# Value panels of attention and memory: two k-tiles of 512 channels in each, four panels adding up in two banks

## The reference, cut to what matters

```python
h = rms_norm(x, norm_w[layer])
proj = jnp.einsum('bsd,de->bse', h, w_in[layer])
(gq, gk, gv, glr, hq, hf, hi, xq, gate) = jnp.split(proj, split_idx, axis=-1)
...
gla_o = chunked_gated_linear_attention(..., split_heads(gv, GLA_HEADS), ...)
hgrn_o = chunked_gated_linear_attention(..., split_heads(hi, HGRN_HEADS), ...)
m = rms_norm(mem, mem_norm_w[layer])
mkv = jnp.einsum('bmd,de->bme', m, w_mem_kv[layer])
mk, mv = jnp.split(mkv, 2, axis=-1)
...
mixed = jnp.concatenate([gla_o, hgrn_o, xo], axis=-1) * jax.nn.silu(gate)
x = x + jnp.einsum('bse,ed->bsd', mixed, w_out[layer])
```

## Time and profile before

| | |
|---|---|
| median of 3 runs | 996.04 us (995.47 to 996.21) |
| profiled execution, its own time | 996.28 us |
| its span | 994.5 us |
| PE busy | 978.4 us (98%), 8087 matmul records |
| PEld busy | 962.3 us (97%) |
| DVE, ACT, POOL busy | 546.6, 492.0, 749.5 us |
| granted PE clock | full (2.4 GHz) in all but the last slice |
| chain that ended last | PE 87%, DVE 6%, ACT 3%, POOL 2% |

### The profile page before, as it was taken

How to read it: one execution, slowest core, us unless ns; L and a number is a source line. 1 busy time by engine, 2 the same in 40 slices (tenths; PEclk the granted TensorE clock), 3 DMA queues, 4 the chain that set the end, 5 groups by cost and what they waited for, 6 DMA issues and landing times.

```text
span 994.5 us, 21475 instructions
## 1 busy us (share of the span) xinstructions
PE 978.4 (98%) x8087; PEld 962.3 (97%) x8087; DVE 546.6 (55%) x976; ACT 492.0 (49%) x767; POOL 749.5 (75%) x586
## 2 busy tenths in 40 slices
PE   9999999999999999999999999999999999999996
PEld 7999999999999999999899899999999999999996
DVE  4945994457644444701783885456647564445113
ACT  6634335456554444544566754532264665454441
POOL 2896757656999888999289855666549549999993
PEclk9999999999999999999999999999999999999998
DMA  9563334343565555566365243443226736666561
GB/s 317 177 195 131 122 126 148 128 128 106 178 194 185 173 169 169 165 180 182 113 187 154 81 128 108 128 128 123 90 86 191 233 108 197 201 191 178 179 182 53
DMA packets 48346, 154.50 MB, mean 155 GB/s; under 512 B 6060, under 2 KB 11188, under 8 KB 48280
## 3 DMA queue, kind: packets, MB, share of 16 engines
q1 hardware_dynamic: 46128, 151.20, 48.9%
q10 hardware_dynamic: 2152, 2.38, 0.7%
HBM read 151.46 MB, written 2.10 MB: 154 GB/s over the span
## 4 chain that ended last, share of the span: by engine, by line
PE 87%; DVE 6%; ACT 3%; POOL 2%; DMA 1%; issue 1%; SPq 0%; DVEq 0%; ACTq 0%; POOLq 0%
PE panel L1846 70%; PE panel L1912 3%; POOL wlo L662 1%; DMA memk<-in_mem_panels 1%; PE aux L2013 1%; PE panel L1883 1%; PE aux L2291 1%; PE aux L2280 1%; PE panel L1948 1%; PE aux L2253 1%; PE aux L2321 1%; PE aux L2330 1%; DVE tmp L1248 1%; PE aux L1920 1%; PE aux L2019 1%
## 5 line engine op out<-in xcount | busy, mean ns | idle before, releaser
L662 POOL TENSOR_TENSOR wlo<-raw,whi 128x512 fp32r<-128x512 f32 x546 | 724.7, 1356 | 222.8 <-ACT whi L759 194.5
L1846 PE MATMUL panel<-xh,whi 128*128 128x256 f32 (+2 forms) x1392 | 400.4, 288 | 1.0 <-POOL wlo L662 0.7
L1846 PE MATMUL panel<-xh,wlo 128*128 128x256 f32 (+2 forms) x1392 | 394.9, 284 | 0.0
L1846 PE MATMUL panel<-xl,whi 128*128 128x256 f32 (+2 forms) x1392 | 394.6, 283 | 0.0
L759 ACT ACTIVATE whi<-raw 128x1024 fp32r<-128x1024 f32 x280 | 293.9, 1054 | 192.4 <-PE panel L1846 155.5
L1846 PEld LDWEIGHTS panel<-xh,whi 128*128 128x128 f32 x1392 | 262.7, 189 | 2.2 <-POOL wlo L662 1.2
L1846 PEld LDWEIGHTS panel<-xh,wlo 128*128 128x128 f32 x1392 | 262.8, 189 | 0.0
L1846 PEld LDWEIGHTS panel<-xl,whi 128*128 128x128 f32 x1392 | 262.0, 188 | 0.2
L1846 PE MATMUL panel<-hh,wlo 128*128 128x272 f32 (+1 forms) x352 | 100.5, 286 | 0.0
L1846 PE MATMUL panel<-hh,whi 128*128 128x272 f32 (+1 forms) x352 | 100.2, 285 | 0.0
L1846 PE MATMUL panel<-hl,whi 128*128 128x272 f32 (+1 forms) x352 | 99.9, 284 | 0.0
(11 more groups left out here) (363 smaller groups left out, 1619.2 us busy)
## 6 DMA issues: line engine op xcount, KB each, us to landing
raw<-in_panels SPq DMA_DIRECT2D x232, 512.0 KB, 3.5
raw<-in_down SPq DMA_DIRECT2D x32, 448.0 KB, 3.3
raw<-in_down SPq DMA_DIRECT2D x16, 512.0 KB, 3.6
memk<-in_mem_panels SPq DMA_DIRECT2D x4, 512.0 KB, 7.7
memx<-in_mem SPq DMA_DIRECT2D x4, 256.0 KB, 5.6
h<-in_x SPq DMA_DIRECT2D x1, 1024.0 KB, 8.6
spill<-h ACTq DMA_DIRECT2D x1, 1024.0 KB, 5.1
h<-spill ACTq DMA_DIRECT2D x1, 1024.0 KB, 6.5
```

What stands on the lines that cost most here:

```text
L662: ins = nc.gpsimd.tensor_tensor(wlo[:, slot, half], raw[:, slot, half], whi[:, slot, half].bitcast(f32), ALU.subtract)
L1846: ins = M(bank[:, 0:w], wt[:, slot, P * t:P * t + P], x[:, kk, c0:c0 + w], start=first and m == 0 and n == 0, stop=last and m == len(pairs ...
```

## The change

A value panel now holds two k-tiles of 512 channels. Four such panels make a group: `part` 0 to 3 brings k-tiles 2·part and 2·part+1, and the group's 512 channels add up in two banks, one for each `rt`, over the whole width of a bank. There are three groups of attention's values and one of the memory's. Each panel has 12 matmuls with 512 moving columns and counts as a pass of its own. The banks are emptied by two 512-column instructions behind the fourth panel. The list `FIRST` is the same. `value_banks` gives the group's banks (0 and 1, then 2 and 3, then 0 and 1), `frees` and the increments of 2 keep the counts of the banks that are skipped, and `mk`'s tiles are drained in the order 2, 3, 0, 1. Steps ("o", i) wait for `value_banks(i // 2)`. The panels are packed accordingly on the host.

```diff
+def value_banks(group):
+    return [IN_O + V + 4 * group + 2 * (group % 2) + rt for rt in range(2)]
...
                 if i < 4:
-                    ins = TT(mk[:, i, :], pb[o % 4][:, 0:ROWS], xrstd[:, 0:ROWS], ALU.mult)
+                    out_wait(o)
+                    TT(mk[:, i, :], pb[o % 4][:, 0:ROWS], xrstd[:, 0:ROWS], ALU.mult).then_inc(bank_free[o % 4], 2 - i // 2)
                 else:
-                    at_i = P * (i // 2 * 2 - 4)
-                    ins = TS(mv[:, i % 2, at_i:at_i + 2 * P], pb[o % 4][:, 0:2 * P], xrstd[:, ROWS + i % 2:ROWS + i % 2 + 1],
-                             None, ALU.mult)
-                ins.then_inc(bank_free[o % 4], 1)
-            for i in range(4):
+                    out_wait(MEM_O + MEMS - 1)
+                    TS(mv[:, i % 2, :], pb[o % 4][:], xrstd[:, ROWS + i % 2:ROWS + i % 2 + 1],
+                       None, ALU.mult).then_inc(bank_free[o % 4], 1)
+            for i in (2, 3, 0, 1):
                 mem_out(i)
...
                 if kk == 3:
-                    mem_out(4)
                     low_panel(IN_P)
-            for i in range(5, 8):
+            for i in (6, 7):
                 mem_out(i)
...
+                    if i >= V:
+                        if i % 4 == 3:
+                            group = (i - V) // 4
+                            out_wait(o)
+                            for rt, b in enumerate(value_banks(group)):
+                                CP(v[:, rt, 512 * group:512 * group + 512], pb[b % 4][:])\
+                                    .then_inc(bank_free[b % 4], 2 if group < 2 else 1)
+                        continue
...
-                        ins = CP(v[:, i % 2, P * (i // 2 * 2 - V):P * (i // 2 * 2 + 2 - V)], bank[:, 0:2 * P])
...
-            def output_rows(o, p, hi_, lo_):
-                if p % 2:
-                    return
...
+            def value_products(banks, p, part, hi_, lo_):
+                for rt, b in enumerate(banks):
+                    for t in range(2):
+                        kk = 2 * part + t
+                        for n, (wt, x) in enumerate(((whi, hi_), (whi, lo_), (wlo, hi_))):
+                            ins = M(pb[b % 4][:], x[:, kk, P * rt:P * rt + P], wt[:, p % RING, 512 * t:512 * t + 512],
+                                    start=kk == 0 and n == 0, stop=kk == KT - 1 and n == 2)
+                ins.then_inc(passed, 1)
+            def output_rows(i):
+                p, part = IN_P + i, i % 4
+                banks = value_banks((i - V) // 4)
+                pe.wait_ge(lo_ready, p + 1)
+                if part == 0:
+                    for b in banks:
+                        pe.wait_ge(bank_free[b % 4], b // 4)
+                value_products(banks, p, part, xh, xl)
...
+            def mem_rows(part):
+                banks = (MEM_O + 6, MEM_O + 7)
+                pe.wait_ge(mem_low, part + 1)
+                pe.wait_ge(lo_ready, V_P + part + 1)
+                if part == 0:
+                    for b in banks:
+                        pe.wait_ge(bank_free[b % 4], b // 4)
+                value_products(banks, V_P + part, part, memgh, memgl)
...
                     if i < 6:
-                        bank_freed(pe, IN_O + V + 2 * i)
-                        bank_freed(pe, IN_O + V + 2 * i + 1)
+                        for b in value_banks(i // 2):
+                            bank_freed(pe, b)
```

More of the change, by code:

```diff
@@ L56, with frees @@
 XQ, GATE, V = 16, 20, 36
+def value_banks(group):
+    return [IN_O + V + 4 * group + 2 * (group % 2) + rt for rt in range(2)]
+def frees(i):
+    return 2 if i in (V - 2, V - 1) else 1
 STAGES = [(2, 1), (2, 1), (2, 1), (4, 2), (4, 2), (1, 2), (1, 0)]
@@ L223, in passes @@
         if i >= 4:
-            panel[V_P + i - 4] = n + (i % 2 == 0)
+            panel[V_P + i - 4] = n
     for i in range(48):
@@ L868, in _ @@
                         out_wait(o)
-                        A(gate[:, i - GATE, :], pb[o % 4][:, 0:ROWS], ACT.Silu).then_inc(bank_free[o % 4], 1)
+                        A(gate[:, i - GATE, :], pb[o % 4][:, 0:ROWS], ACT.Silu).then_inc(bank_free[o % 4], frees(i))
                 if kind == "level" and step[1] >= LAST_HALF:
@@ L1232, in mem_out @@
                 dve.wait_ge(rstd_ready, 1)
-                out_wait(o)
                 if i < 4:
-                    ins = TT(mk[:, i, :], pb[o % 4][:, 0:ROWS], xrstd[:, 0:ROWS], ALU.mult)
-                else:
-                    at_i = P * (i // 2 * 2 - 4)
-                    ins = TS(mv[:, i % 2, at_i:at_i + 2 * P], pb[o % 4][:, 0:2 * P], xrstd[:, ROWS + i % 2:ROWS + i % 2 + 1],
-                             None, ALU.mult)
-                ins.then_inc(bank_free[o % 4], 1)
-            for i in range(4):
+                    out_wait(o)
+                    TT(mk[:, i, :], pb[o % 4][:, 0:ROWS], xrstd[:, 0:ROWS], ALU.mult).then_inc(bank_free[o % 4], 2 - i // 2)
+                else:
+                    out_wait(MEM_O + MEMS - 1)
+                    TS(mv[:, i % 2, :], pb[o % 4][:], xrstd[:, ROWS + i % 2:ROWS + i % 2 + 1],
+                       None, ALU.mult).then_inc(bank_free[o % 4], 1)
+            for i in (2, 3, 0, 1):
                 mem_out(i)
@@ L1323, in _ @@
                         ins = CP(q[:, i - 8, :], bank[:, 0:ROWS])
-                    elif i < GATE:
+                    else:
                         continue
-                    else:
-                        ins = CP(v[:, i % 2, P * (i // 2 * 2 - V):P * (i // 2 * 2 + 2 - V)], bank[:, 0:2 * P])
                     ins.then_inc(bank_free[o % 4], 1)
@@ L1899, in total @@
                 M(bank[:, 0:W[n]], ones[:], sq[:, 1, 0:W[n]], start=False, stop=True).then_inc(aux_full, 1)
-            def output_rows(o, p, hi_, lo_):
-                if p % 2:
-                    return
[L1906 to L1910, removed]
-                        for n, (wt, x) in enumerate(((whi, hi_), (whi, lo_), (wlo, hi_))):
-                            ins = M(pb[(o + rt) % 4][:, 0:2 * P], x[:, kk, P * rt:P * rt + P],
-                                    wt[:, r:r + 2, P * kk:P * kk + P], start=kk == 0 and n == 0, stop=kk == KT - 1 and n == 2)
-                ins.then_inc(passed, 2)
+            def value_products(banks, p, part, hi_, lo_):
+                for rt, b in enumerate(banks):
+                    for t in range(2):
+                        kk = 2 * part + t
+                        for n, (wt, x) in enumerate(((whi, hi_), (whi, lo_), (wlo, hi_))):
+                            ins = M(pb[b % 4][:], x[:, kk, P * rt:P * rt + P], wt[:, p % RING, 512 * t:512 * t + 512],
[9 more added lines that the diff above has]
+                value_products(banks, p, part, xh, xl)
             def transposes(bank, src, rows):
@@ L1975, in _ @@
                     norm_stat(i - 2)
-            mem_rows(4)
-            mem_rows(6)
+            for part in range(4):
+                mem_rows(part)
             pe.wait_ge(more_in, 11 * 16)
@@ L1986, in _ @@
                     if i >= V:
-                        output_rows(IN_O + i, IN_P + i, xh, xl)
+                        output_rows(i)
                     else:
@@ L2059, in _ @@
                             aux_freed(pe, AUX[("probs", u)])
-                        for o in range(4, 8):
+                        for o in (MEM_O + 6, MEM_O + 7):
                             bank_freed(pe, o)
                     if i < 6:
-                        bank_freed(pe, IN_O + V + 2 * i)
-                        bank_freed(pe, IN_O + V + 2 * i + 1)
+                        for b in value_banks(i // 2):
+                            bank_freed(pe, b)
                     for e in range(2):
@@ L2438, with values @@
     gates = pack(gates, KT)
+    def values(w_):
+        p = pack(w_, KT)
+        return p.reshape(-1, 4, P, 4, 2, P).transpose(0, 3, 2, 4, 1, 5).reshape(-1, P, 1024)
     def halves(w_):
@@ L2466 @@
     w_out = np.stack([w_out[i, :, half] for i, half in W_OUT])
-    mem_panels = pack(x["w_mem_kv"], KT)
-    panels = np.concatenate([mem_panels[4:]] + [pack(p, KT) for p in (hf, gk, gq, hq, xq, gate, gv, hi)]
-                            + [w_out, up(x["ffn1_wi_2"]), np.stack(mixer), pack(x["w_out_2"], KT), up(x["ffn2_wi_2"])])
+    mem_panels = pack(x["w_mem_kv"][:, 0:512], KT)
+    panels = np.concatenate([values(x["w_mem_kv"][:, 512:])] + [pack(p, KT) for p in (hf, gk, gq, hq, xq, gate)]
+                            + [values(gv), values(hi)] + [w_out, up(x["ffn1_wi_2"]), np.stack(mixer), pack(x["w_out_2"], KT), up(x["ffn2_wi_2"])])
     down = np.concatenate([pack(x["ffn1_wo_2"], FT), pack(x["ffn2_wo_2"], FT)])
@@ L2482 @@
              "dt_bias": np.broadcast_to(x["dn_dt_bias_2"].reshape(1, 8), (P, 8))}
-    arrays = {"panels": panels, "mem_panels": mem_panels[:4], "down": down, "x": rows(x["x"]), "mem": rows(x["mem"]), "meta": rows(x["meta_tokens_2"]),
```

(1 more changed line is left out.)

## The result

| | before | changed |
|---|---|---|
| median | 996.1 us (995.47 to 997.31, 7 runs) | 999.41 us (999.22 to 1000.36, 7 runs) |
| span of the profiled execution | 994.5 us | 997.8 us |
| PE busy, matmul records | 978.4 us, 8087 | 978.1 us, 7895 |
| DVE busy, instructions | 546.6 us, 976 | 539.3 us, 968 |

The ratio is 1.0031, with a 95% interval from 1.0021 to 1.0041. The changed kernel is slower by 3.3 us, by the medians as by the spans. Timed again on another chip its ratio was 1.0027 (1.0012 to 1.0043). The forecast was 998.8 us, 2.8 us over before.

A forecast was written before the change was run, and what follows sets the result against it. The prediction took PE to bound the kernel, so time it spends or saves is nearly time at the end. Products −0.8, copies +4.0 and start −0.4 gave +2.8 us on 996.04, so 998.8 us, range 996.7 to 1000.3.

The forecast's parts named there:

- Products: Attention's value products: 144 matmuls of 512 columns at 231 ns replace pairs of 256 columns at 236.6, saving 0.8 us.
- the two slopes: Cost of 16 more columns, 256 to 272: 7.8 ns in the feed-forward loops, 6.7 ns in the loops behind them.
- the bounds of 225 and 243: Time of a 512-column value matmul extrapolated from 256 and 272 columns: saving 1.7 us at 225 ns, losing 0.9 at 243.
- Copies: PE waits for DVE's copies of both banks: 0.75 us before ("o", 0), 1.62 before ("o", 2) and ("o", 4), 4.0 us altogether.
- The start: Memory's values: DVE splits panel 4 earlier, POOL goes on 0.39 us earlier, output 4 starts earlier, gaining 0.4 us.
- The shift without a sign: Between 99.93 and 129.69 us, PE's wait for DVE may move up to 1 us either way; taken as 0.
- The sum: Whole kernel: −0.8 for products, +4.0 for copies, −0.4 for the start, +2.8 us, giving 998.8 us.
- The fixed excess (225 ns): Rival: value matmuls' excess is fixed per matmul, saving 1.7 us; sum +1.9, 998.0 us; chance 0.24.
- the vanishing one (216): Rival: value matmuls of 512 columns take 216 ns, saving 3.0 us; sum +0.6, 996.7 us; chance 0.10.
- that rival's +4.5 us: Rival: DVE reaches the value copies late, or 512 columns take 243 ns; +4.5 or more, 1000.7 us; chance 0.08.
- the smoother release of ring slots: Ring slots come free panel by panel, not by pairs, helping ACT and POOL; nothing on PE waits there, costed at nothing.

The follow-up runs named there:

- series of widths: Not the kernel's computation: only back-to-back fp32r matmuls, 48 of each width from 256 to 512 columns; 118.3 ns at 256, 231.3 at 512 with tiles 272 words apart.
- r1_changed_again: The changed kernel as it is, timed again on another chip beside the kernel before: 1000.44 us, ratio 1.0027.
- e4_before_waits: The kernel before, its 256-column matmuls and order kept, but steps (o, 0), (o, 2), (o, 4) wait for the last finished pair's copies: 998.59 us, ratio 1.0016.
- e5_memory_alone: The kernel before with the change made to the memory's values alone, attention's values as before: 995.89 us, ratio 0.9996.
- the earlier order: The changed kernel with each pair of value panels from V+4 on one step earlier in the list: 995.83 us, ratio 0.9989; again 996.07 us, 0.9992.

## Why the prediction was right, point by point

**Products.** Forecast 231 ns and a saving of 0.8 us. In the changed kernel the six pairs take 33.5 us and took 34.0, so the saving was 0.5 us, 232.9 ns per matmul. That the cost lies between fixed and proportional is borne out by the series of widths. That it lies so near the middle was luck in part: no row ahead of the run singled out 231, the mean of the two slopes was 234, and a slope over 16 columns is too short for more than the bounds of 225 and 243. The memory's 512-column matmuls, taken as 231 too, took 235.6 ns (48 from 23.48 to 34.79), and the 256-column ones 120.8. That cost nothing, since POOL set the time of output 4.

**Copies.** Forecast 0.75, 1.62 and 1.62 us; measured 0.83, 1.71 and 1.64. Each piece held: DVE starts 0.43 to 0.51 us after the last matmul's start (0.42 forecast), two copies take 1.29 or 1.30 us (1.28), and the handover to PE is 0.14 us (0.15). The sum of 4.0 became 4.2. The eight transposes ahead of ("o", 0) (line 1920 of the kernel before) have one record each and not two, 16 records for 16 transposes in its trace.

**The start.** Forecast 0.4 us, measured 0.23. The mechanism was right: DVE's split started 0.29 us earlier and not 0.39, since the chain in front of it was 0.07 to 0.1 us late in this execution (the scaling of x started at 24.29 and not at 24.22), and POOL took 0.05 us longer for its six halves. The other traces tell the gain from such shifts. Counted from the first of the memory's value products, the split starts after 8.97 to 8.99 us in the four traces of the old form and after 8.59 to 8.61 in the seven of the new one, so 0.38 us earlier, and output 4 after 23.24 to 23.31 and 22.90 to 23.04 us.

**The shift without a sign.** Between 99 and 130 us PE's wait stayed what it was; PE was 0.23 us ahead when it went in and 0.28 when it came out. The 1 us kept for it was not needed here, but the shift exists: in r1_changed_again, e4_before_waits and e5_memory_alone PE gained 0.38 to 0.39 us between 112 and 130 us, so the same kernel shows it in one execution and not in another.

**The sum.** −0.5 + 4.2 − 0.3 = +3.4 us at 228 us, and nothing after that gave any of it back: the last matmul is 3.4 us late. The forecast's +2.8 fell short because all three terms erred to the same side by 0.1 to 0.3 us. So the mechanism and its largest term were right, the small terms were all a little too kind, and none of them was large enough to matter.

**The rivals.** The fixed excess (225 ns) and the vanishing one (216) are out for attention's values, by 232.9 ns in the kernel and 231.3 in the series of widths. With tiles 256 words apart the series alone would not have told fixed (226.5) from what it gave, 227.5. The copies as such cost no more than forecast; for that rival's +4.5 us the time would be 1000.5 and not 1000.7 us. That the smoother release of ring slots is worth nothing was true in this order. It is not in another: with the pairs one step earlier it is worth 0.6 us. The prediction did not weigh that.

## What to carry to other kernels

Before products are regrouped so that several panels finish an output together, look at who reads it and what stands between: the saving per instruction is small (5 ns of 237 here), and the 144 matmuls saved 0.5 us where one wait for two copies lost 1.7. The remedy was in the order and not in the products, and it brought the time back to that of the kernel before and not shown to be under it. And a swap that serves the waiting engine first can starve it, where a third engine takes both results from one queue in order.

## What the runs showed of the hardware that was not expected

- An fp32r matmul back to back costs more than its columns. With nothing else running, 256 columns took 118.3 ns with stationary tiles 272 words apart and 119.8 with tiles 256 words apart; 448 columns took 202.3 and 206.5, and at 384 and 512 it was the other way round (175.4 against 173.4, 231.3 against 227.5). In the kernel the memory's 512-column matmuls, with tiles 256 words apart, took 235.6 ns. So the distance of the tiles, or something that goes with it, changes the cost, in neither direction for good. The cause is open.
- A stationary tile of 32 columns in place of 128 saved 4.1 ns at 256 moving columns and nothing at 512 (231.3 in both). Whether the weight load shows through under the shorter stream was not tested further.
- The granted clock separates the two groups of runs. These are the stretches from 500 to 502 us of the changed kernel in its first profiled execution and in r1_changed_again (window, its length, PE busy, the clock, DMA share, GB/s):

```profile
500.00:502.00 2.00, 2.00 (x18) 1.00 0.66 242
```

```profile
500.00:502.00 2.00, 2.00 (x11) 0.50 0.62 231
```

  In both, PE had stood still for 1.2 us between 496 and 500 us (busy 1.33 and 1.51 of 2 us each in the first). In the second the clock then fell to 1.2 GHz, matmuls of 272 columns came 226 to 227 ns apart and not 122 to 130, and PE lost 1.4 us by it. The two executions of the earlier order differ in the same way from 496.6 us on, by 1.2 us. At the lower clock 272 columns are 226.7 ns, so the excess of the matmuls does not show there.
- By the Trainium skill, "TensorE: Matmul & The Clock Gate", section "Back-to-back issue gap", the gap of an isolated matmul is N/2.4 + 2.5 ns, an estimate of 215.8 ns at 512 columns, and a stream of weight loads and matmuls of 512 columns comes to about 131 ns each. The traces agree with neither for fp32r: no run of 512 columns here came under 227.5 ns.
